# Last LayerNorm of a hybrid decoder layer: row sums of some tiles on ScalarE, three tiles scaled and shifted on VectorE

## The reference

```python
def layer_norm(x, g, b):
    mu = xf.mean(-1, keepdims=True)
    var = jnp.square(xf - mu).mean(-1, keepdims=True)
    return (xf - mu) * lax.rsqrt(var + LN_EPS) * g + b
...
x = layer_norm(DEEPNORM_ALPHA * x + grouped_moe(x, ...), ln2_g, ln2_b)
```

## Time and profile before

| | |
|---|---|
| median of 3 runs | 1360.35 us (1359.79 to 1361.69) |
| the profiled execution, its own time | 1360.65 us |
| its span, first to last instruction | 1359.0 us |
| mean granted PE clock | 0.941 |
| busy: PE / DVE / ACT / POOL | 88% / 66% / 34% / 35% of the span |
| DMA | 222.84 MB, mean 164 GB/s |
| last LayerNorm: first statistics to last shift | 1298.02 to 1353.01 us |

### The profile page before, as it was taken

How to read it: one execution, slowest core, us unless ns; L and a number is a source line. 1 busy time by engine, 2 the same in 40 slices (tenths; PEclk the granted TensorE clock), 3 DMA queues, 4 the chain that set the end, 5 groups by cost and what they waited for, 6 DMA issues and landing times. The chain is left out here.

```text
span 1359.0 us, 22638 instructions
## 1 busy us (share of the span) xinstructions
PE 1196.5 (88%) x6653; PEld 955.5 (70%) x6654; DVE 895.2 (66%) x1980; ACT 458.8 (34%) x679; POOL 475.1 (35%) x553
## 2 busy tenths in 40 slices
PE   7999999799879777999999259999999999999910
PEld 6997999778767544888888257767767767767600
DVE  3452876468877564466667667777777777777586
ACT  4221110110012451222221125556556555556433
POOL 3008850200110014322222023545545545445267
PEclk9999999899989988999999579999999999999965
DMA  8555342564154322433332546787977777644484
GB/s 258 173 198 161 142 125 65 155 228 175 64 165 147 111 87 67 153 111 112 119 119 97 224 163 195 214 245 225 253 201 227 210 211 216 145 98 98 117 309 174
DMA packets 112874, 222.84 MB, mean 164 GB/s; under 512 B 51304, under 2 KB 68280, under 8 KB 103568
## 3 DMA queue, kind: packets, MB, share of 16 engines
q1 hardware_dynamic: 96368, 164.86, 36.0%
q0 software_dynamic: 15408, 55.12, 17.3%
q10 hardware_dynamic: 1040, 2.10, 0.4%
HBM read 144.34 MB, written 77.58 MB: 163 GB/s over the span
## 5 line engine op out<-in xcount | busy, mean ns | idle before, releaser
L2030 DVE TENSOR_TENSOR wgu<-w_raw,wgu (+1 forms) x192 | 226.0, 1219 | 52.5 <-ACT wgu L2117 52.4
L2211 PE MATMUL p_gu<-wgu,xg_high 128*128 x768 | 254.2, 412 | 4.5 <-DVE xg_low L2023 4.5
L2117 ACT CAST wgu<-w_raw (+1 forms) x192 | 187.1, 1050 | 19.3 <-SPq L1845 16.6
L2211 PEld LDWEIGHTS p_gu<-wgu,xg_high 128*128 128x128 f32 x768 | 145.1, 190 | 59.0 <-issue 31.3
L2234 PE MATMUL p_d<-wd,ht 128*128 x384 | 174.9, 598 | 1.8 <-DVE ht L2044 1.0
L2211 PE MATMUL p_gu<-wgu,xg_low 128*128 x384 | 151.8, 395 | 0.0
L2234 PEld LDWEIGHTS p_d<-wd,ht 128*128 128x128 f32 x384 | 69.0, 189 | 71.5 <-issue 71.2
L1710 PE MATMUL p_out<-w_out_high,mixt_high 128*128 128x512 f32 (+1 forms) x272 | 108.2, 398 | 12.4 <-POOL mixt_low L1487 12.4
L1710 PE MATMUL p_out<-w_out_high,mixt_low 128*128 128x512 f32 (+1 forms) x272 | 106.6, 392 | 0.0
L1710 PE MATMUL p_out<-w_out_low,mixt_high 128*128 128x512 f32 (+1 forms) x272 | 106.4, 391 | 0.0
L1914 POOL TENSOR_TENSOR spare_e<-nothing 128x1 f32<-128x1 f32 x48 | 9.2, 192 | 233.2 <-DVE yo L2050 233.2
(11 more groups left out here) (434 smaller groups left out, 2677.6 us busy)
## 6 DMA issues: line engine op xcount, KB each, us to landing
w_raw<-in_w_gate SPq DMA_DIRECT2D x16, 1024.0 KB, 4.8
w_raw<-in_w_up SPq DMA_DIRECT2D x16, 1024.0 KB, 7.8
wd<-in_w_down SPq DMA_DIRECT2D x16, 1024.0 KB, 4.9
acc_rows<-ax SPq DMA_DIRECT2D x18, 512.0 KB, 5.7
xin<-in_x_prompt SPq DMA_DIRECT2D x16, 512.0 KB, 6.3
sq<-sq_mats SPq DMA_DIRECT2D x16, 512.0 KB
z<-in_x_prompt SPq DMA_DIRECT2D x16, 512.0 KB, 4.1
x_rows<-x SPq DMA_DIRECT2D x16, 512.0 KB, 4.9
```

The costliest lines, as they stand in the source:

```text
L2030: low = tt(wgu[:, slot, 1, at], raw[:, slot, at], wgu[:, slot, 0, at].bitcast(F32), ALU.subtract)
L2117: nc.scalar.copy(wgu[:, slot, 0, at], raw[:, slot, at]).then_inc(hi_set, 1)
L2211: mm = t.matmul(pg[b][:, :, :], x[:, b, k, :], w[h][:, k], start=(k == 0 and x is xh and h == 0), stop=(k == KD - 1 and x is xl))
```

## The change

A string `KINDS` gives each position a kind. N tiles go as before. For S and U tiles ACT takes the statistics: a `Copy` with an accumulated sum, a multiplication of the sum by -1/1024 (`low2`, minus the mean), and a `Square` with `low2` as bias and an accumulated sum (`ssq2`); both passes write their elements to a scratch tile `junk`. DVE then only makes `var2` from `ssq2`, and centres with `low2`. A U tile is moreover scaled and shifted on DVE in one `scalar_tensor_tensor` whose two tensor inputs both lie in SBUF, and ACT and POOL skip it. ACT now follows the pairs: statistics of a pair, then the scaling of the pair before. The title given to the change speaks of ten tiles; the string holds five S (positions 1, 5, 8, 11, 14) and three U (3, 9, 15), which is eight, and nine N.

```diff
+            sum2, low2, ssq2 = (sb(n, [P, TILES], where=rows) for n in ("sum2", "low2", "ssq2"))
...
+            junk = sb("junk", [P, D], where=Place(nc, base + 35 * KB))
...
+            KINDS = "NSNUNSNNSUNSNNSUN"
...
@@ SP
                 for n, c in enumerate(ORDER):
-                    sp.wait_ge(shifted, n + 1)
+                    sp.wait_ge((shifted, shifted_dve)[KINDS[n] == "U"], KINDS[:n + 1].count("U") if KINDS[n] == "U" else n + 1 - KINDS[:n].count("U"))
@@ POOL
                 def shift(n, c):
+                    if KINDS[n] == "U":
+                        return
                     r = tokens(c)
-                    gp.wait_ge(scaled, n + 1)
+                    gp.wait_ge(scaled, n + 1 - KINDS[:n].count("U"))
@@ DVE
                 def stats(n, c):
                     r = tokens(c)
+                    if KINDS[n] != "N":
+                        dve.wait_ge(ssq_set, n + 1 - KINDS[:n + 1].count("N"))
+                        ts(var2[0:r, n:n + 1], ssq2[0:r, n:n + 1], 1.0 / D, EPS, ALU.mult, ALU.add).then_inc(var_set, 1)
+                        return
...
                 def centre(n, c):
                     r = tokens(c)
-                    stt(zi[0:r, c, :], zi[0:r, c, :], ag2[0:r, n, 0:1], pt_xx[0:r].rearrange("p h k n -> p (h k n)"),
-                        ALU.subtract, ALU.mult).then_inc(centred, 1)
+                    row = zi[0:r, c, :]
+                    g = pt_xx[0:r].rearrange("p h k n -> p (h k n)")
+                    if KINDS[n] == "N":
+                        stt(row, row, ag2[0:r, n, 0:1], g, ALU.subtract, ALU.mult).then_inc(centred, 1)
+                    else:
+                        stt(row, row, low2[0:r, n:n + 1], g, ALU.add, ALU.mult).then_inc(centred, 1)
+                    if KINDS[n] == "U":
+                        dve.wait_ge(centred, n + 1)
+                        dve.wait_ge(rstd_set, n // 2 + 1)
+                        stt(row, row, rstd2[0:r, n:n + 1], b2_row[0:r, :], ALU.mult, ALU.add).then_inc(shifted_dve, 1)
...
                     if n == 0:
                         dve.wait_ge(g_set, 2)
+                        dve.wait_ge(row2_in, 32)
@@ ACT
-                for n, c in enumerate(ORDER):
+                def act_stats(n, c):
+                    if KINDS[n] == "N":
+                        return
+                    r, m = tokens(c), n + 1 - KINDS[:n + 1].count("N")
+                    act.wait_ge(acc_in[c], 16)
+                    nc.scalar.activation(junk[0:r, :], zi[0:r, c, :], ACT.Copy, accum_out=sum2[0:r, n:n + 1]).then_inc(low_set, 1)
+                    act.wait_ge(low_set, 2 * m - 1)
+                    nc.scalar.mul(low2[0:r, n:n + 1], sum2[0:r, n:n + 1], -1.0 / D).then_inc(low_set, 1)
+                    act.wait_ge(low_set, 2 * m)
+                    nc.scalar.activation(junk[0:r, :], zi[0:r, c, :], ACT.Square, bias=low2[0:r, n:n + 1],
+                                         accum_out=ssq2[0:r, n:n + 1]).then_inc(ssq_set, 1)
+                    act.wait_ge(ssq_set, m)
+
+                def scale(n, c):
+                    if KINDS[n] == "U":
+                        return
                     r = tokens(c)
                     act.wait_ge(rstd_set, n // 2 + 1)
                     act.wait_ge(centred, n + 1)
                     nc.scalar.mul(zi[0:r, c, :], zi[0:r, c, :], rstd2[0:r, n:n + 1]).then_inc(scaled, 1)
+
+                for n, cs in PAIRED:
+                    for k, c in enumerate(cs):
+                        act_stats(n + k, c)
+                    if n:
+                        for k in range(2):
+                            scale(n - 2 + k, ORDER[n - 2 + k])
+                scale(TILES - 1, ORDER[TILES - 1])
```

More of the change, by code:

```diff
@@ L1812, in hybrid_step @@
              yo_dve, te_set, row2_in, half_set, var_set, rstd_set, g_set, centred, scaled, shifted, y_stored,
-             fdch) = sems("""nothing_set cnt_prod tables_set2 hot_set list_prod
+             fdch, shifted_dve, low_set, ssq_set) = sems("""nothing_set cnt_prod tables_set2 hot_set list_prod
              lists_set raw_ready wd_ready w_high_set prep_done edch gi_set si_set xg_turned xg_act xg_dve gu_prod silu_set hh_set h_turned
              ht_set d_prod yo_act yo_dve te_set row2_in half2_set var2_set rstd2_set g_set centred scaled shifted
-             y_stored fdch""")
+             y_stored fdch shifted_dve low_set ssq_set""")
             acc_in = [phase_sem(f"acc_in{c}") for c in range(TILES)]
@@ L1821, in hybrid_step @@
             ORDER = [CH, *range(CH)]
+            KINDS = "NSNUNSNNSUNSNNSUN"
+            assert len(KINDS) == TILES
             PAIRED = [(n, ORDER[n:n + 2]) for n in range(0, TILES, 2)]
```

## The result

| | before | changed |
|---|---|---|
| median of 6 runs | 1361.02 us (1359.20 to 1363.42) | 1370.08 us (1367.51 to 1372.57) |
| ratio, with its 95% interval | | 1.0058 (1.0046 to 1.0071) |
| profiled execution's span | 1359.0 us | 1367.3 us |
| last LayerNorm, first statistics to end of last shift | 1298.02 to 1353.02: 55.00 us | 1296.77 to 1361.22: 64.45 us |

The ratio on 1361.0 us is +7.9 us, the medians differ by 9.1, the spans by 8.3. The LayerNorm alone grew by 9.45 us; the rest of the span came out 1.2 us shorter, because everything ahead of the LayerNorm happened to end earlier in this execution.

What follows compares the result with a forecast made beforehand. DVE was taken to set the last LayerNorm's pace, and with the change a loop of ACT and DVE waits; stepping the queues gave 1364.1 - 1353.1 = +11.0 us, so 1371.3 us on the median, range 1367 to 1377.

Steps and rivals of the forecast that it cites:

- The first case: Last LayerNorm: ACT and DVE wait on each other, DVE ahead of POOL at the SBUF port; +11.0 us, chance 0.68.
- The ring: ACT's statistics queue behind scalings awaiting DVE's centrings, themselves behind variances awaiting ACT; 6.6 us where a pair took 5.64.
- a set: ACT's statistics of one tile: copy pass, small multiplication, square pass, sums and waits; 2.86 us, or 2.50 with sums free.
- The prediction's marks: Profile signs: DVE's variance waits for ACT some 22 us, POOL idles between pairs, last shift ends near 1364.
- The size: Last LayerNorm's last shift ends at 1364.1 against 1353.1 stepped for the kernel before: +11.0 us.
- one turn: ACT's statistics of one tile, handover, small variance, two centrings, handover, last scaling: 6.6 us after a one-ACT-tile pair.
- The end of the path: Position 16 after position 15's U instruction: centring 1.27, scaling 1.15, shift 2.35 us and two handovers, ending at 1364.10.
- Loads: The last two loads land by 1314.4; DVE reaches those tiles after 1340, so even a slower load is covered.
- The shared port: U instructions and POOL's shifts both read two SBUF tensors and hold each other back; without it +10.2 us.
- Accumulator read: On ACT each accumulated sum might be a separate instruction, as the skill says for VectorE; 0.18 us charged twice per tile.
- Rival 2: ACT's work fits its idle time and DVE is relieved: -8.6 us, 1351.8; break-even at 1.49 us per tile's statistics; chance 0.05.
- Rival 3: The change does less than its title says, eight tiles rather than ten; eight were priced; no chance of its own given.

Runs made afterwards that it cites:

- e1_ahead: Changed kernel with only ACT's queue order altered, each pair's statistics one pair earlier: LayerNorm 55.30 us (changed kernel 64.45), ratio 1.0007 to the kernel before.
- e2_s_only: Changed kernel with its three U tiles made N, leaving five tiles' statistics on ACT: LayerNorm 61.61 us, ratio 1.0048 to the kernel before.
- e10_short_square: Changed kernel with ACT's squares over 16 columns instead of 1024, for timing only: LayerNorm 57.73 us, ratio 1.0010 to the kernel before.
- e12_ring_psum: Changed kernel with beta for the U instructions in PSUM, copied by ACT: LayerNorm 63.88 us, ratio 1.0070 to the kernel before.
- e9_late_copy: Changed kernel with a 128x512 copy from PSUM on DVE ahead of each U instruction: LayerNorm 68.98 us, ratio 1.0098 to the kernel before.
- e5_ahead_psum: Changed kernel with ACT's statistics one pair earlier and beta for U instructions in PSUM: LayerNorm 49.73 us, ratio 0.9960 to the kernel before.
- e7_best_psum: Changed kernel, ACT's statistics one pair earlier, beta in PSUM, four S and four U tiles: LayerNorm 43.18 us, ratio 0.9913 to the kernel before.
- e6_best_port: Changed kernel, ACT's statistics one pair earlier, beta in SBUF, six S and four late U tiles: LayerNorm 46.70 us, ratio 0.9945 to the kernel before.
- e8_later_u: Changed kernel with a 128x1024 DVE memset ahead of each U instruction: LayerNorm 66.72 us; ran once, no ratio.

## Why the prediction was right, and by how much its terms were off

The forecast was 1371.3 us with a range of 1367 to 1377, slower with 0.92; measured were 1370.08 and +0.58%. The first case happened, by its own steps. The nearness of the two times is in part luck: the LayerNorm grew by 1.55 us less than forecast, but the median of the kernel before came out 0.7 us above the one that I added to, once more runs were taken.

- **The ring.** Shown by e1_ahead (order alone takes 9.2 us back), e2_s_only (6.6 us without any U tile) and e10_short_square (a set counts eight times). The prediction's marks stood in the profile: DVE ahead of the small variance idle for 1.92, 0.86, 2.19, 3.83 and 2.54 us at positions 1, 3, 5, 8 and 9 (forecast 2.3, 1.1, 2.5, 4.1, 2.8), 19.9 in all (22).
- **The size.** The LayerNorm was forecast to grow by 11.0 us and grew by 9.45 (the runs by 7.9 by the ratio). The mis-sized term is the price of a set: "2.86 us", measured 2.69. I charged 0.18 for each accumulated sum on top of the pass; it is an instruction of 0.19 us, but it overlaps the pass by 0.10, so each adds 0.09. Eight sets make 8 x 0.17 = 1.4 of the 1.55 us. (The parts listed for one turn add up to 6.62 and those from 5 to 8 to 13.58, where I carried 6.58 and 13.53; that is rounding beside the set.) Step by step, from the start of one set to that of the next:

| from, to | forecast | measured |
|---|---|---|
| position 1 to 3 (one set) | 2.85 | 2.69 |
| 3 to 5 (one turn) | 6.58 | 6.36 |
| 5 to 8 (over a pair of two N) | 13.53 | 13.31 |
| 8 to 11 (two sets) | 9.43 | 9.05 |
| 11 to 14 | 13.53 | 13.31 |
| 14 to the last shift's end | 19.18 | 18.82 |

- **The end of the path.** I let the last shift wait for ACT's last scaling. I had left out that POOL still had the power of position 16 and the shift of 14 to do, and that the power would be held up beside the U instruction of position 15 (1.55 us). The last shift waited for those. It began 0.26 us after the scaling's end, where a handover is 0.08, so this step was worth some 0.2 us.
- **Loads.** DVE took up the last two tiles in the kernel before at 1336.71 and 1340.72, and not both after 1340. They had landed by about 1314.4, so nothing hangs on it.

- **The shared port.** "Without it the sum would be +10.2", so 0.8 us: e12_ring_psum measured 0.6. That DVE would be first at positions 3 and 9 was right; the margin was 0.11 us by the recorded starts, where I said 0.08. The U instruction of position 15 took 1.85 us, 0.56 more than alone (forecast 0.7). The rule quoted from the Trainium skill ("SBUF — State Buffer", section "Summary: rules for kernel authors") is borne out by e9_late_copy. It isn't the whole of it: "the second one to issue fully blocks until the first finishes" would let DVE in at 1313.31 in e1_ahead, and it came in at 1316.29, after two more of POOL's instructions.
- **Accumulator read.** The page "VectorE: DVE Perf Modes" (the Trainium skill, section "Two Vector instructions with no wait between them") states two instructions for VectorE only; the trace shows the same on ScalarE (`ACTIVATION_READ_ACCUMULATOR`, 0.19 us, behind each of the two passes). The set was not the 2.86 us even so, because of the overlap.
- **Rival 2** (ACT's work fits its idle time, 1351.8 us) did not happen, for the reason given, the order of ACT's queue. e5_ahead_psum and e7_best_psum show that the idle time it counted on was real: once the ring was open and the port free, the LayerNorm was 5.3 and 11.8 us shorter than before. Its break-even was a set of 1.49 us; by the measured sizes it is 2.69 - 9.45 / 8 = 1.51. What the prediction did not see is that opening the ring alone would bring nothing, because the port then takes it back.
- **Rival 3** (fewer tiles than the change's words): eight sets, as priced.

## What to carry to other kernels

When work is moved to an idle engine, ask first what stands ahead of it in that engine's queue and whom that waits for: idle time made of waits can be used only by work queued before the wait. The ring showed in this profile as two engines that each wait for the other by like sums (20.6 and 19.9 us), with none of them busy throughout; the order of instructions in one queue opened it. Then look for the next coupling before expecting the gain, here two engines reading two SBUF tensors each.

## What the runs showed of the hardware that I had not expected

- A DVE instruction that waits for the shared port can be passed over by POOL instructions behind the one that it waits for: by two in e1_ahead (6.00 us for 1.28 us of work), by one in e6_best_port (5.43). At position 9 of e1_ahead it did get in between two back-to-back shifts (2.27 us, and the two shifts took 5.64). In the two cases of being passed over the U instruction had begun 0.40 and 0.30 us after the start of the shift that it waited for; where it got its turn behind that shift with more of POOL's work queued, it had begun 0.97 us after it or later (among them e6_best_port at position 16, e1_ahead at 9 and 15, the changed kernel at 15). No run varies this alone, so what decides stays open.
- A DVE memset into SBUF, with no SBUF input at all, can hold POOL's `tensor_tensor` up: 4.31 us in place of 2.34 with 0.91 of memset and 1.16 of a U instruction beside it (e8_later_u, position 3, memset 0.13 us after the shift's recorded start). It did not hold up a shift that had run for 1.8 us, nor wait for it (position 15). So at position 3 the shift's recorded start was not yet its hold on the port. A U instruction that began 0.50 us after the shift had to wait (e9_late_copy).
- A 128x16 ACT square with a per-partition bias took 0.31 us, against 0.18 for the 128x16 sigmoid in the earlier trace rows.
